# Hybrid decoder step on one core: the second output block's weights split around the last merge steps, state decay issued one place ahead, expert ranks ahead of two subtractions, and the third row part subtracted by VectorE

## What is computed

```
x  = x + (g_a*o_a + g_b*o_b + g_c*o_c) @ w_o          # merge and output projection
s_new = s0 * decay + outer(k, u)                        # state of 8 samples, for each of 8 heads
h2 = RMSNorm(x)
group, two experts = router(h2)                         # top 1 of 4 groups, top 2 of its 8 experts
x  = x + sum over the chosen experts of w * down(silu(gate(h2)) * up(h2))
y  = RMSNorm(x)
```

## Time and profile before

| | |
|---|---|
| median of 3 runs | 1405.93 us (1404.48 to 1407.48) |
| the profiled execution, its own time | 1402.81 us |
| its span, first to last instruction | 1401.0 us |
| PE busy | 1295.0 us, 92% |
| VectorE busy | 487.5 us, 35% |
| ScalarE busy | 450.9 us, 32% |
| GpSimd busy | 138.9 us, 10% |
| granted TensorE clock, mean | 0.983 of full |

### The profile page before, as it was taken

How to read it: one execution, slowest core, us unless ns; L and a number is a source line. 1 busy time by engine, 2 the same in 40 slices (tenths; PEclk the granted TensorE clock), 3 DMA queues, 4 the chain that set the end, 5 groups by cost and what they waited for, 6 DMA issues and landing times.

```text
span 1401.0 us, 24089 instructions
## 1 busy us (share of the span) xinstructions
PE 1295.0 (92%) x10413; PEld 1009.9 (72%) x10413; DVE 487.5 (35%) x883; ACT 450.9 (32%) x776; POOL 138.9 (10%) x206
## 2 busy tenths in 40 slices
PE   3999999999999998989999779899999999999997
PEld 3999988788999997879999678544445444455436
DVE  6332243433345656723345685201010010010013
ACT  5532225343243565534445554111101110111112
POOL 2320000000122211101001011001000000000010
PEclk9999999999999999989999999999999999999999
DMA  5235238542261233341113347699999999999982
GB/s 210 86 104 161 106 120 327 186 158 84 92 218 61 82 112 101 94 132 51 52 39 141 120 151 315 249 392 430 428 433 429 432 431 431 431 428 432 428 325 67
DMA packets 66588, 317.62 MB, mean 227 GB/s; under 512 B 29939, under 2 KB 38515, under 8 KB 44229
## 3 DMA queue, kind: packets, MB, share of 16 engines
q1 hardware_dynamic: 64205, 312.54, 56.7%
q0 software_dynamic: 2304, 3.94, 0.7%
HBM read 295.80 MB, written 25.10 MB: 229 GB/s over the span
## 4 chain that ended last, share of the span: by engine, by line
PE 68%; DMA 17%; DVE 7%; ACT 6%; issue 2%; SPq 1%; POOL 0%; DVEq 0%; ACTq 0%
PE pp L880 33%; PE pp L1056 15%; DMA e_up<-in_w_up 13%; PE pp L1046 4%; PE pp L930 2%; DMA e_down<-in_w_down 1%; PE pp L1215 1%; PE pp L1235 1%; DMA raw<-in_w_blk 1%; PE pp L1243 1%; DVE w_l L2012 1%; PE pp L1358 1%; ACT w_h L1456 1%; PE pp L1400 1%; PE pp L1410 1%
## 5 line engine op out<-in xcount | busy, mean ns | idle before, releaser
L880 PE MATMUL pp<-ht_h,w_h 128*128 128x260 f32 x1280 | 270.2, 293 | 9.4 <-DVE ht_l L2134 9.4
L880 PE MATMUL pp<-ht_h,w_l 128*128 128x260 f32 x1280 | 260.0, 285 | 0.0
L880 PE MATMUL pp<-ht_l,w_h 128*128 128x260 f32 x1280 | 260.0, 285 | 0.0
L880 PEld LDWEIGHTS pp<-ht_h,w_h 128*128 128x128 f32 x1280 | 200.2, 192 | 15.5 <-issue 14.2
L880 PEld LDWEIGHTS pp<-ht_h,w_l 128*128 128x128 f32 x1280 | 199.8, 191 | 0.0
L880 PEld LDWEIGHTS pp<-ht_l,w_h 128*128 128x128 f32 x1280 | 199.8, 191 | 0.0
L2012 DVE TENSOR_TENSOR w_l<-raw,w_h 128x2048 fp32r<-128x2048 f32 x52 | 120.9, 2325 | 108.1 <-ACT w_h L1456 108.0
L1056 PE MATMUL pp<-e_down,act_t 128*64 128x512 f32 x512 | 115.1, 602 | 20.1 <-ACT act_t L1791 17.4
L1456 ACT ACTIVATE w_h<-raw 128x2048 fp32r<-128x2048 f32 x52 | 99.5, 1914 | 54.9 <-PE pp L880 51.6
L1056 PE MATMUL pp<-e_up,xt 128*64 128x512 f32 x512 | 113.1, 594 | 4.4 <-DMA e_up<-in_w_up 4.2
L1056 PE MATMUL pp<-e_gate,xt 128*64 128x512 f32 x512 | 112.6, 592 | 1.1 <-ACT xt L1777 1.1
(11 more groups left out here) (448 smaller groups left out, 1666.8 us busy)
## 6 DMA issues: line engine op xcount, KB each, us to landing
e_up<-in_w_up SPq DMA_DIRECT2D x16, 4096.0 KB
e_gate<-in_w_gate SPq DMA_DIRECT2D x16, 4096.0 KB, 19.8
e_down<-in_w_down SPq DMA_DIRECT2D x32, 2048.0 KB, 13.8
raw<-in_w_blk SPq DMA_DIRECT2D x52, 1024.0 KB, 5.2
kv_ring<-in_cache_k SPq DMA_DIRECT2D x8, 1024.0 KB, 6.8
kv_ring<-in_cache_v SPq DMA_DIRECT2D x8, 1024.0 KB, 4.9
s_ring<-in_state_gdn SPq DMA_DIRECT2D x16, 512.0 KB, 5.2
y_rows<-zero_y SPq DMA_DIRECT2D x10, 416.0 KB
```

The lines of the kernel that those rows point to most:

```text
L880: last = mm(dst, w_[:, k, cs], x_[:, k, ts], start=(k == 0 and q == 0), stop=(k == KD - 1 and q == 2))
```

## The change

It reorders the schedule and moves some small work between engines:

- The single entry of tile 96 becomes two. The first half stands ahead of `fin` 2 to 7; ScalarE's split of block 49 and SP's load of block 50 go with it, and PE's fused multiplication too. The second half stands right behind `fin_end`; VectorE's split of block 49 and its `x1` of tile 96 go with that, followed by tile 97. The `f_prep` 0 and 1 now stand ahead of `sd_diag` 1.
- The decay of a head's state is an entry of its own, `sd_decay`, issued behind the add of the head before.
- `rank` moves ahead of `h_sub` 0 2 and `h_in` 3. The entries `h_sub` 1 t for t = 1 to 4 go: VectorE's `low(t)` subtracts part 1 while it reads PSUM, for t = 1, 2, 3, 4. ScalarE no longer copies part 2 of t = 2.
- `gain_d` moves from k = 2 to k = 6; two of the four constants there go to GpSimd, behind its own constants.

```
+    gap(63, ("tile", WO_TILE, 0, 2))
     for h, g in enumerate((62, 62, 63, 63, 63, 63, 63, 63)):
         gap(g, ("fin", h))
-    gap(63, ("fin_end",))
+    gap(63, ("fin_end",), ("tile", WO_TILE, 1, 2), ("tile", WO_TILE + 1, 0, 1))
...
-    out += [("sd_diag", 0), ("sd_diag", 1), ("w_r_split",), ("tile", WO_TILE, 0, 1), ("tile", WO_TILE + 1, 0, 1),
-            ("f_prep", 0), ("f_prep", 1)]
+    out += [("sd_diag", 0), ("w_r_split",), ("f_prep", 0), ("f_prep", 1), ("sd_decay", 0), ("sd_diag", 1)]
...
-                out += [("sd_outer", h)] + ([("sd_diag", h + 2)] if h + 2 < NH else [])
+                out += [("sd_outer", h)] + ([("sd_decay", h + 1)] if h + 1 < NH else [])
+                out += [("sd_diag", h + 2)] if h + 2 < NH else []
     out += [("h_in", 0), ("r_mm", KD - 1), ("f_norm",), ("router",), ("h_sub", 0, 0), ("h_in", 1), ("h_sub", 1, 0),
-            ("h_in", 2), ("h_sub", 0, 1), ("h_sub", 0, 2), ("h_in", 3), ("h_sub", 1, 1), ("rank",), ("h_sub", 1, 2),
-            ("h_sub", 0, 3), ("h_in", 4), ("h_sub", 1, 3), ("h_sub", 0, 4), ("h_sub", 1, 4), ("moe",), ("final",)]
+            ("h_in", 2), ("h_sub", 0, 1), ("rank",), ("h_sub", 0, 2), ("h_in", 3), ("h_sub", 0, 3), ("h_in", 4), ("h_sub", 0, 4),
+            ("moe",), ("final",)]
...
# PE, "moe"
-                    pe.wait_ge(ht_lo, 3)
-                    pe.wait_ge(ht_part, 2)
+                    pe.wait_ge(ht_lo, 4)
+                    pe.wait_ge(ht_part, 1)
...
# ScalarE, "router"
-                    part(2, 2)
...
# GpSimd, "f_table"
+                    for i, name in ((3, "tok_hi"), (4, "tok_lo")):
+                        nc.gpsimd.tensor_copy(vals[:, :, :, i:i + 1].rearrange("p t e o -> p t (e o)"),
+                                              const(name, TT).rearrange("p (t o) -> p t o", o=1).to_broadcast([TT, NT, NE]))\
+                            .then_inc(h_consts, 1)
...
# VectorE, tile
-                if j % 2 == 0 and part == 0 and b + 1 < NBLK:
+                if j % 2 == 0 and part == (j == WO_TILE) and b + 1 < NBLK:
                     weights_lo(b + 1)
...
# VectorE
-                elif e == "sd_outer":
+                elif e == "sd_decay":
                     h = ev[1]
                     own = s1_ring[h % 4]
                     dve.wait_ge(ring_loaded[h % 4], 64 + 16 * (h // 4 + 3))
                     link(tt(own[:], own[:], s_bc[:, 1, :, h:h + 1].to_broadcast([128, NS, 128]), ALU.mult))
+                elif e == "sd_outer":
+                    h = ev[1]
+                    own = s1_ring[h % 4]
                     mmed(dve, ev)
                     flat = own[:].rearrange("p (a b) n -> p a (b n)", a=2)
                     tt(flat, pp[UNIT[ev]][:], flat, ALU.add).then_inc(sd_new, 1)
...
-                    if k == 2:
+                    if k == KD - 2:
                         tt(gain_d[:], const("ident").rearrange("p (o n) -> p o n", o=1).to_broadcast([128, KD, 128]),
...
-                        copy(val(3), per_token("tok_hi"))
-                        copy(val(4), per_token("tok_lo"))
...
                     def low(t):
-                        dve.wait_ge(ht_sub[1], t + 1)
-                        copy(h2p[2][:, t, :].rearrange("p (a n) -> p a n", a=2), pp[H_UNIT[t]][0:TT]).then_inc(ht_lo, 1)
+                        dve.wait_ge(ht_mid, t + 1)
+                        tt(h2p[2][:, t, :].rearrange("p (a n) -> p a n", a=2), pp[H_UNIT[t]][0:TT],
+                           h2p[1][:, t, :].rearrange("p (a n) -> p a n", a=2), ALU.subtract).then_inc(ht_lo, 1)
...
                     one_hot(0)
+                    low(2)
                     low(3)
```

More of the change, by code:

```diff
@@ L827, in tile @@
             def tile(j, part, parts):
-                if j == WO_TILE + 1:
+                if j == WO_TILE + 1 or (j == WO_TILE and part):
                     return
@@ L2099, in val @@
                 return vals[:, :, 0:n, i:i + 1].rearrange("p t e o -> p t (e o)")
-            def per_token(name):
-                return const(name, TT).rearrange("p (t o) -> p t o", o=1).to_broadcast([TT, NT, NE])
             def late_lo(h):
@@ L2416, in _ @@
                             .then_inc(gain_ready, 1)
-                    if k == KD - 2:
                         copy(strict_b[:], const("strict", TT)[:, 0:TT])
                         copy(ones_b[:], const("ones", TT))
-                        copy(val(3), per_token("tok_hi"))
-                        copy(val(4), per_token("tok_lo"))
                 elif e == "router":
@@ L2554, in _ @@
                     dve.wait_ge(rstd_parts, 8)
+                    dve.wait_ge(h_consts, 4)
                     ts_(rows_of[1][:], const("ones")[:, 0:1], 4096.0, None, ALU.mult).then_inc(no_rows, 1)
```

## The result

| | runs | median us | lowest to highest |
|---|---|---|---|
| kernel before, same session | 4 | 1406.7 | 1404.48 to 1407.62 |
| changed kernel | 4 | 1387.46 | 1387.11 to 1388.12 |

The ratio is 0.9872, with an interval of 0.9859 to 0.9884: the change makes the kernel faster by 19.2 us, where 13.3 were forecast. So two questions stand: what the change is worth, and what made the first figure so low. The profiled execution took 1387.21 us with a span of 1385.4.

What follows compares the result with a forecast made beforehand. The bound was PE's path up to the second `e_gate` issue at 895.12, not the weight stream. Stage 12.9 plus router 1.6 less clock 1.2 gives 13.3 us: 1405.93 to 1392.6, range 1389.0 to 1398.0.

Steps and rivals of the forecast that it cites:

- the low end of the range: Whole execution: no clock loss, 1391.4, less 1.5 by which runs stray from their median, and router 0.7 more: 1389.0.
- The middle of the forecast: Whole execution: 13.3 us off the median shown, 1405.93, giving 1392.6; the profiled execution should become 1389.5; chance 0.58.
- rival 2: Output projection: GpSimd's sum of squares blocks VectorE's adds, gain 10.3 us, 1395.6; chance 0.11.
- 5.9 + 12.5 - 5.6: Output projection stage: earlier tile 98, plus time that was not work, less remaining waits and restarts; given as 12.9 us.
- The start of tile 98: Output projection: with block 49 split early, PE starts tile 98 at 789.55, 5.9 us earlier.
- The remaining waits: Output projection: PE still waits 1.8, 2.1 and 1.4 us at outer products 1, 4 and 5.
- The clock's term: PE behind the three remaining waits: one in four brings 1.2 GHz at 1.6 us, 1.2 us lost.
- Rival 1: PE's clock falls after each remaining wait, 3 x 1.6 lost: gain 9.7 us, 1396.2; chance 0.18.
- decays all near 1.22: Sign of being right: VectorE's state decays, moved behind the previous add, take about 1.22 us, not 2.33.
- The router: Router from ranks to gather: moved ranks and dropped subtractions give 1.6 us; 0 if VectorE is late, 2.3 at most.
- the third rival: Router part gives nothing, since VectorE does four subtractions and the rank arithmetic: 1394.2; chance 0.08.
- Rivals 4 and 5: Weight stream sets the end anyway, 1405.9, chance 0.03; decays wait for ring buffer reloads, slower, 1412.3, chance 0.02.

Runs made afterwards that it cites:

- before again: The kernel before, unchanged and timed again: 1405.11 us against 1404.86, ratio 1.0005.
- split alone: Kernel before with only the early split of block 49 (and load of block 50); decays, constants and router stay: 1401.67 us, ratio 0.9977.
- decay alone: Kernel before with only each head's state decay issued one place ahead: 1397.37 us, ratio 0.9948.
- router alone: Kernel before with only the router edits (`rank` moved, `low(t)` subtracts, one PE subtraction gone): 1403.42 us, ratio 0.9993.
- constants alone: Kernel before with only `gain_d` at k = 6 and `tok_hi`, `tok_lo` copied by GpSimd: 1405.44 us, ratio 1.0004.
- filled, before: Kernel before with 50 added matmuls, overwritten unread, in PE's idle time ahead of tile 98: 1406.08 us, ratio 1.0.
- changed, second: The changed kernel, unedited, timed in a second session: 1390.82 us over 6 runs, ratio 0.9896 to the kernel before.
- changed, third: The changed kernel, unedited, timed in a third session: 1389.35 us over 5 runs, ratio 0.9895 to the kernel before.
- changed, router as before: Changed kernel with its router edits taken back, so early split and decay together, constants' part included: 1391.16 us, ratio 0.9889 to the kernel before.
- `gain_d` back: Changed kernel with `gain_d` made at k = 2 again instead of k = 6: 1394.77 us, ratio 0.9927 to the kernel before.
- changed, filled: Changed kernel with added matmuls ahead of outer products 1 and 5 (the second misplaced; the long wait is at 4): 1392.27 us, ratio 0.9893.
- order altered: Changed kernel with state 0's decay earlier, `u_diag` 1 and block 51's low weights later: 1383.52 us, ratio 0.9852 to the kernel before.

## Why the prediction was wrong

Each profiled span cuts into four parts, all read from the timelines: up to VectorE's last `mr_l` (upstream); from there to its first `h2p` copy (the stage); from there to the second `e_gate` (the router and first gate matmuls); and the rest. The last column is the time at 1.2 GHz within the stage, from the trace's record of the granted clock. The early split reaches into the end of the upstream part, but does not alter it: from PE's first fused matmul to the last `mr_l` all fourteen profiles have 10.8 us.

| kernel | upstream | stage | router | rest | low clock in the stage |
|---|---|---|---|---|---|
| before | 784.8 | 68.9 | 41.4 | 505.9 | 10.2 |
| before again | 786.6 | 69.0 | 41.4 | 504.3 | 10.2 |
| split alone | 788.1 | 66.7 | 42.2 | 504.0 | 13.7 |
| decay alone | 788.5 | 63.2 | 42.1 | 504.3 | 10.2 |
| router alone | 787.8 | 69.0 | 40.5 | 504.1 | 10.2 |
| constants alone | 787.1 | 69.4 | 41.0 | 505.9 | 13.7 |
| filled, before | 788.4 | 68.9 | 41.3 | 505.7 | 6.8 |
| changed | 785.1 | 57.1 | 39.4 | 503.8 | 6.8 |
| changed, second | 786.5 | 57.0 | 39.1 | 505.9 | 3.4 |
| changed, third | 786.9 | 57.0 | 39.0 | 506.3 | 3.4 |
| changed, router as before | 788.5 | 57.0 | 39.6 | 506.1 | 3.4 |
| `gain_d` back | 787.6 | 60.3 | 39.0 | 506.0 | 6.8 |
| changed, filled | 788.4 | 57.1 | 39.4 | 505.9 | 3.4 |
| order altered | 786.3 | 52.1 | 39.0 | 504.1 | 0 |

**The step that failed is the low end of the range**, "less the 1.5 by which runs stray from their median". It took the parts of the execution that the change does not touch to be the same in both kernels but for 1.5 us. They are not. The upstream part lies between 784.8 and 788.5, and goes with the low clock in it (20 to 24 us where it ends before 787.2, 27 to 31 where it ends later). The rest is 503.8 to 504.3 or 505.7 to 506.3, whatever the kernel; between the profile before and the first one after, 1.7 of the 2.05 are the last down matmuls:

```profile
1341.14 7.09 PE L1057 MATMUL pp<-e_down,act_t 128*64 128x512 f32 x32 [2.43 <-DMA e_down<-in_w_down]
```
```profile
1342.64 8.78 PE L1057 MATMUL pp<-e_down,act_t 128*64 128x512 f32 x32 [2.80 <-DMA e_down<-in_w_down]
```

The first row is of the changed kernel, the second of its second session; the same 32 matmuls took 8.78 in the profile before. Here too it is the clock: these matmuls take 8.78 in all eight profiles with the long rest and 7.09 in all six with the short one, and only the eight have a stretch of 1.2 GHz there. In the first session the changed kernel had the short form of both parts: 1.5 to 1.8 us upstream and 2.1 to 2.5 in the rest below its two repeats. That is 3.2 to 3.8 us between profiled spans that are alike in stage and router, and it covers the distance from 1387.46 to the 1390.8 and 1389.4 measured later.

The granted clock of that session's four executions was 0.986 to 0.988, and 0.981 to 0.986 in the eleven later ones. Why the clock was so high in all four is not settled; no run tests it.

The middle of the forecast carried a like assumption. 1392.6 stood 3.1 above the forecast for a profiled execution, because the profile before lay that far below its median; the profile after lay 0.25 below its own. That is 2.85 of the 5.1 us between 1392.6 and 1387.46. The other 2.3 are the profiled span, shorter by 15.6 instead of 13.3: 2.05 in the rest, 0.1 in the stage, 0.4 in the router, less 0.2 upstream. With 5 us of such play, 1391.4 (no clock loss) less 5, the range should have begun near 1386.

Three sums of the forecast were slightly off, none of which decides: 1391.4 - 1.5 - 0.7 is 1389.2 and not 1389.0; rival 2 with three adds at 1.11 gives 10.0 and 1395.9, not 10.3 and 1395.6; and 5.9 + 12.5 - 5.6 is 12.8, not 12.9.

**The start of tile 98** was right: forecast 789.55, measured 789.52, with 0.56 of idle time where 0.84 had been walked. That it agrees to the tenth is luck, since the last `mr_l` came 0.24 later than in the profile before.

**The remaining waits** were right in place and slightly high in size: forecast 1.8, 2.1 and 1.4 at outer products 1, 4 and 5; measured 1.54, 1.80 and none, then 1.60, 1.84 and 1.07 in the second session, whose row for number 5 is

```profile
823.13 0.72 PE L1306 MATMUL pp<-u_diag,k_st 72*128 72x512 f32 x2 [1.07 <-DVE small L2411]
```

`r_mm` 6 starts at 839.12 and ends at 839.8 (by the 0.71 of the forecast), where 838.5 + 1.2 for the clock had been summed.

**The clock's term** was near in size, 1.2 forecast, and too simple in kind. The changed kernel had two low stretches in the first profile and one in the next two, yet its stage took 57.1 and 57.0 us. Such a stretch lasts 3.4 us in the record. The one behind outer product 1 costs about 1.5 us each time (5.69 us to number 2, against 4.16 in the filled kernel). The one behind number 4 costs 0.1, since PE would otherwise have waited 1.07 at number 5: VectorE, held up by block 51, frees the unit late whether PE is fast or slow. Elsewhere in the stage a wait does not swallow a stretch. VectorE's row there starts at the end of PE's tile, so it comes later with PE: in the filled kernel before, the stretch behind outer product 1 cost 1.5 although the wait at number 3 stood behind it, unchanged at 1.92. Both filled kernels won 1.5 us behind the filled wait and lost it in the stretch that followed.

Rival 1, low clock behind each of three waits at 1.6, came true for two waits of two in the first profile and for one of three in the next two, and its price of 4.8 was never paid. The Trainium skill (TensorE: Matmul & The Clock Gate, HAM oscillation) describes a loop that is throttled at every wait for data, each of them longer than the 2 us or so of matmuls between them. Here the wait of 6.8 us ahead of tile 98 had low clock behind it in all five profiles that have it unfilled, while the waits of 1.5 to 2.0 us were followed by low clock in some profiles and not in others at the same place.

**GpSimd and the adds** (rival 2) is refuted: all eight adds took 1.216 to 1.224. The Trainium skill (SBUF — State Buffer, SBUF: two separate sides) says that a VectorE operation with two SBUF inputs can be blocked by a GpSimd operation that reads SBUF, which started first; the trace agrees, at 2.33 for such a decay and 1.22 for the add, whose one operand is in PSUM, beside the same GpSimd instruction. The forecast's "decays all near 1.22" held for seven of eight: state 0's starts 0.11 us behind a sum of GpSimd and takes 2.33.

**The router** was mis-sized: 1.6 forecast, 41.4 less 39.0 to 39.4, thus 2.0 to 2.4, measured. Most of it is not the edits': the pair without them already stands at 39.6. It goes with less low clock in this part, 3.4 to 6.8 us in every kernel that has both early parts against 10.2 before (with the constants alone 6.8, and 41.0 for the part); that this is the cause is only argued. The edits' own share is 0.3 to 0.6 us beside the pair, and 0.9 in the kernel before, where they did bring the gather 1.65 us forward and low clock on the gather took 0.8 back. So that the whole part came out near the forecast is luck; the third rival (no gain) fits the edits' share beside the pair better.

**The sum by stages** is then 11.9 for the stage (11.7 forecast, 12.9 less 1.2) and 2.2 for the router: 14.1, against 13.3 forecast and 14.9 and 15.3 measured by the medians of the repeats. **Rivals 4 and 5** are refuted: no decay waited for a transfer, and the stream stood still ahead of the second `e_gate`, at 0 GB/s from 872 to 880 us.

**The parts do not add.** Alone they take 2.3 (split), 5.8 (decay) and nothing (constants) off the stage, 8.1 in all; together 11.9. The run with `gain_d` put back says where the difference lies: with split, decay and everything else in, it has 8.7 off, nearly the 8.1 of the single parts, and moving `gain_d` gives the rest, 3.3 beside the third repeat. That instruction stands in VectorE's row ahead of outer product 0's add, and so in front of outer product 1. Without the early parts, the 1.0 us that its move won was lost to low clock further on; with them, it takes away 2.2 us of wait and 3.4 us of low clock. The place of `sd_diag` 1 is in all of the combined runs and was not tested alone. My expectations for single parts missed both ways: the split gave 3.2 us for 6.8, the decay 7.5 for 4.8 to 6.4.

## What to carry to other kernels

Where two engines pace each other, price an edit with the others in, and by undoing it from the final kernel as well: the constants' part was worth nothing alone, and `gain_d`'s place 3.3 us of the stage at the end. Don't expect matmuls put into a wait to buy clock back: twice they won 1.5 us there and the next low stretch took it. Shortening VectorE's row removed waits and low clock together in the last experiment (4.9 us off the stage, granted clock 1.00 in it). And take the range's ends from how far stretches that no edit touches differ between executions, not from the change's own terms alone; here that was 3.7 us ahead of the stage and 2.5 behind it.

## What the hardware showed unexpectedly

Up to `mr_l`, where the edits alter nothing, the profiles had 20 to 31 us of 1.2 GHz, worth 3.7 us, and one stretch more or less under the last 32 down matmuls made them 8.78 or 7.09 us. Busy time added in a wait moved the low stretch to the next wait rather than removing it (from behind outer product 1 to behind number 4), and one session's four executions lay within 1.0 us of each other while later sessions of the same file spread over 4 and 6 us.
